# MoE weights of a decoder-layer step: gate/up in two 4 MB slots, four neighbouring rows per partition, down in 2 MB pieces

## The reference, cut to what matters

```
logits = x2d @ w_router + b_router
top_v, top_i = lax.top_k(logits, 4)          # 4 of 32 experts per token
gates = softmax(top_v)
h = xb @ w_gate_up[e] + b_gate_up[e]          # (tokens, 1024) @ (1024, 2048)
x_glu, x_lin = min(h[..., ::2], 7), clip(h[..., 1::2], -7, 7)
h = x_glu * sigmoid(1.702 * x_glu) * (x_lin + 1)
y += gate * (h @ w_down[e] + b_down[e])       # (tokens, 1024) @ (1024, 1024)
```

## Time and profile before

| | |
|---|---|
| median of 3 runs | 1138.27 us (1138.12 to 1141.05) |
| profiled execution, span from first to last instruction | 1140.5 us |
| its own device time | not shown apart; of the three times, 1141.05 us is the one that holds the span |
| TensorE busy | 1027.2 us, 90% |
| VectorE, ScalarE busy | 403.0 us, 206.3 us |
| DMA | 426.10 MB, mean 374 GB/s |
| chain that ended last | PE 80%, DVE 8%, DMA 5%, issue 3%, ACT 3% |

### The profile page before, as it was taken

How to read it: one execution, slowest core, us unless ns; L and a number is a source line. 1 busy time by engine, 2 the same in 40 slices (tenths; PEclk the granted TensorE clock), 3 DMA queues, 4 the chain that set the end, 5 groups by cost and what they waited for, 6 DMA issues and landing times.

```text
span 1140.5 us, 17017 instructions
## 1 busy us (share of the span) xinstructions
PE 1027.2 (90%) x6428; PEld 432.8 (38%) x6428; DVE 403.0 (35%) x886; ACT 206.3 (18%) x440; POOL 7.0 (1%) x7
## 2 busy tenths in 40 slices
PE   6987999999988998899887988789999999999995
PEld 5756875333332323232332233223333333333332
DVE  6978645231322232223222133213333333222223
ACT  4576332111111111111101011101011111111110
POOL 1000000000000000000000000000000000000000
PEclk9978999999999999999999999989999999999998
DMA  9513871999999999999999999999999999999993
GB/s 357 170 47 98 357 308 50 390 423 421 407 417 420 420 421 421 420 419 421 421 421 419 422 420 421 422 420 422 421 422 422 422 421 422 422 422 421 422 420 134
DMA packets 65633, 426.10 MB, mean 374 GB/s; under 512 B 9988, under 2 KB 13188, under 8 KB 15648
## 3 DMA queue, kind: packets, MB, share of 16 engines
q1 hardware_dynamic: 63792, 422.88, 90.2%
q10 hardware_dynamic: 1728, 2.11, 0.5%
q0 software_dynamic: 48, 0.15, 0.0%
HBM read 419.86 MB, written 2.51 MB: 370 GB/s over the span
## 4 chain that ended last, share of the span: by engine, by line
PE 80%; DVE 8%; DMA 5%; issue 3%; ACT 3%; SPq 1%; ACTq 1%; DVEq 0%
PE banks L489 76%; DMA gu_ring<-w_gu_dram 5%; DVE xT L1873 2%; DVE raw L1827 1%; PE banks L855 1%; PE banks L817 1%; ACT gath L1267 1%; PE banks L908 1%; DVE hl L1839 1%; DVE hT L1844 1%; SPq L324 1%; ACT s_p L1170 0%; PE banks L862 0%; PE banks L915 0%; PE banks L624 0%
## 5 line engine op out<-in xcount | busy, mean ns | idle before, releaser
L489 PE MATMUL banks<-gu_ring,xe 128*64 128x512 f32 x1408 | 324.2, 603 | 4.2 <-DMA gu_ring<-w_gu_dram 4.0
L1873 DVE TENSOR_TENSOR xT<-xT,banks 128x576 f32<-128x576 f32 x132 | 93.7, 751 | 488.9 <-PE banks L489 488.9
L489 PEld LDWEIGHTS banks<-gu_ring,xe 128*64 128x64 f32 x1408 | 95.1, 137 | 198.0 <-issue 189.0
L489 PE MATMUL banks<-dn_ring,hT 128*64 128x512 f32 x704 | 157.7, 596 | 3.5 <-DVE hT L1844 3.5
L489 PE MATMUL banks<-gu_ring,xe_s 128*32 128x512 f32 x896 | 110.2, 599 | 11.5 <-issue 6.0
L489 PEld LDWEIGHTS banks<-dn_ring,hT 128*64 128x64 f32 x704 | 47.8, 137 | 94.6 <-issue 88.7
L489 PE MATMUL banks<-gT,ye 64*128 64x288 f32 x352 | 57.8, 439 | 13.4 <-DVE xT L1873 12.7
L1282 ACT ACTIVATE raw<-banks 128x512 f32<-128x512 f32 x22 | 13.1, 597 | 295.5 <-PE banks L489 295.5
L489 PE MATMUL banks<-x_tok,oh 96*64 96x512 f32 x264 | 63.2, 615 | 0.1
L489 PE MATMUL banks<-dn_ring,hT_s 128*32 128x256 f32 x896 | 55.3, 394 | 2.7 <-ACT xe_s L1301 2.7
L1827 DVE COPY raw<-banks 128x512 f32<-128x512 f32 x22 | 15.2, 692 | 109.1 <-PE banks L489 109.1
(11 more groups left out here) (344 smaller groups left out, 838.3 us busy)
## 6 DMA issues: line engine op xcount, KB each, us to landing
gu_ring<-w_gu_dram SPq DMA_DIRECT2D x256, 1024.0 KB, 23.6
dn_ring<-w_dn_dram SPq DMA_DIRECT2D x128, 1024.0 KB, 20.6
w_out<-w_out_dram SPq DMA_DIRECT2D x2, 2048.0 KB, 10.3
w_in<-w_in_dram SPq DMA_DIRECT2D x3, 1024.0 KB, 16.2
w_in<-w_in_dram SPq DMA_DIRECT2D x4, 512.0 KB, 9.7
W<-W1c SPq DMA_DIRECT2D x16, 128.0 KB, 2.3
w_glu<-w_glu_dram SPq DMA_DIRECT2D x1, 2048.0 KB, 8.7
xT<-xT_dram SPq DMA_DIRECT2D x2, 576.0 KB, 5.6
```

The lines of the kernel that those rows point to most:

```text
L489: return nc.tensor.matmul(out, lhsT, rhs, start=start, stop=stop, **kw)
L1873: X.tensor_tensor(two, two, pair[(1, 3)[n % 2]].rearrange("p (h f) -> p h f", h=2)[:, :, 0:T], ALU.add).then_inc(S("acc_done"), 1)
```

## The change

The gate/up weights of an expert come in two pieces of 4 MB instead of eight of 1 MB. Slot k holds rows 512k to 512k+511 of the weights, and partition p of it the four neighbouring rows 512k+4p to 512k+4p+3, which lie one behind the other in DRAM: 32 KB per partition. TensorE contracts row i of all partitions at a time, so a chunk is now every fourth row. Down comes in two pieces of 2 MB with 16 KB per partition, four rows each. TensorE waits for a gate/up slot at chunks 0 and 4 and for a down piece at every second; SP refills a slot after its fourth chunk, a down piece after its second. Places 0 and 1 still get their gate/up weights in 1 MB pieces of 8 KB per partition, and those of place 1 don't wait for `order_ready` any more.

So that the operands match, ScalarE writes `x_tok` with its columns permuted, the copies of the hidden values (`raw`, `raw_s`) put their blocks in another order, and the transposes of the hidden values read every second column. The gate/up bias is permuted once, by four matmuls (`turn_gate_bias`) and a ScalarE copy early in the kernel. The seven early semaphores of `w_in` become their own.

```diff
+GU_SLOTS = 2
+GU_ROWS = KT // GU_SLOTS
...
-    gu_ring = [sb(f"gu_ring{k}", [2 * D], GU + k * 8192) for k in range(8)]
-    dn_ring = [sb(f"dn_ring{k}", [2, D], DN + k * 8192) for k in range(8)]
+    gu_ring = [sb(f"gu_ring{k}", [GU_ROWS, 2 * D], GU + k * GU_ROWS * 8192) for k in range(GU_SLOTS)]
+    dn_ring = [sb(f"dn_ring{k}", [4, D], DN + k * 16384) for k in range(4)]
...
     def load_gu(sp, x, k):
-        sp.dma_start(gu_ring[k][:], a["w_gu"][bass.ds(x, 1), k].rearrange("o p f -> (o p) f")).then_inc(gu_in[k], 16)
...
+        src = a["w_gu"][bass.ds(x, 1), GU_ROWS * k:GU_ROWS * (k + 1)].rearrange("o k p f -> (o k p) f").rearrange(
+            "(p i) f -> p i f", i=GU_ROWS)
+        sp.dma_start(gu_ring[k][:], src).then_inc(gu_in[k], 16)
...
         def gu(x, p_before):
-            for k in range(8):
-                sp.wait_ge(S("gu_used"), p_before * 8 + (k + 1))
+            for k in range(GU_SLOTS):
+                sp.wait_ge(S("gu_used"), p_before * 8 + GU_ROWS * (k + 1))
                 load_gu(sp, x, k)
 
+        def dn(x, p_before, j):
+            for h in range(2):
+                sp.wait_ge(S("dn_used"), p_before * 4 + 2 * (h + 1))
+                load_dn(sp, x, h, j)
+
+        for r in range(KT):
+            sp.wait_ge(S("gu_used"), r + 1)
+            first_gu(sp, 1, [r])
         sp.wait_ge(S("order_ready"), 1)
...
         turn_b(0)
+        turn_gate_bias()
...
             for k in chunks:
-                pe.wait_ge(gu_in[k], p * 16 + (16 + W_IN[k]))
+                slot, i = gu_ring[k // GU_ROWS], k % GU_ROWS
+                if i == 0:
+                    pe.wait_ge(gu_in[k // GU_ROWS], gu_filled(p, k // GU_ROWS))
...
+        def hidden_cols(ap, m):
+
+            return ap.rearrange("p (k n i) -> p k i n", k=2, i=2)[:, m % 2, m // 2]
...
-                    last = pe.transpose(pb[2 + part][:, c * P:(c + 1) * P], raw[:, part, c * P:(c + 1) * P], ident[:])
+                    last = pe.transpose(pb[2 + part][:, c * P:(c + 1) * P], hidden_cols(raw[:, part], c), ident[:])
...
-                pe.wait_ge(dn_in[4 * j + c], fill * 16)
+                if c % 2 == 0:
+                    pe.wait_ge(dn_in[2 * j + c // 2], fill * 16)
...
-            A(x_tok[u // 2][0:MT, (u % 2) * HALF:(u % 2 + 1) * HALF], pb[XB[u]][0:MT, :], ACT.Copy,
+            half = x_tok[u // 2][0:MT, (u % 2) * HALF:(u % 2 + 1) * HALF]
+            A(half.rearrange("p (i f) -> p f i", i=GU_ROWS),
+              pb[XB[u]][0:MT, :].rearrange("p (f i) -> p f i", i=GU_ROWS), ACT.Copy,
...
-            A(raw[:, 0], pb[0][:], ACT.Copy).then_inc(S("g_copied"), 1)
+            A(blocks_out(raw[:, 0]), blocks_in(pb[0]), ACT.Copy).then_inc(S("g_copied"), 1)
```

More of the change, by code:

```diff
@@ L289, in build @@
         S(n)
[L290 to L293, removed]
+    wu_in, wq_in = [S(f"wu_in{c}") for c in range(CT)], [S(f"wq_in{c}") for c in range(3)]
+    gu_in = [S(f"gu_in{k}") for k in range(GU_SLOTS)]
+    dn_in = [S(f"dn_in{k}") for k in range(4)]
     order = {"dve": 0, "act": 0}
@@ L320, in build, with gu_rows, dn_rows, load_dn @@
     assert at == 42
-    def load_gu(sp, x, k):
-        sp.dma_start(gu_ring[k][:], a["w_gu"][bass.ds(x, 1), k].rearrange("o p f -> (o p) f")).then_inc(gu_in[k], 16)
[L326 to L333, removed]
+    def gu_rows(x, k):
+        return a["w_gu"][x, GU_ROWS * k:GU_ROWS * (k + 1)].rearrange("k p f -> (k p) f").rearrange(
+            "(p i) f -> p i f", i=GU_ROWS)
+    def dn_rows(x, h):
+        return a["w_dn"][x, 2 * h:2 * h + 2].rearrange("c p k f -> (c p k) f").rearrange("(p i) f -> p i f", i=4)
+    def load_gu(sp, x, k):
+        src = a["w_gu"][bass.ds(x, 1), GU_ROWS * k:GU_ROWS * (k + 1)].rearrange("o k p f -> (o k p) f").rearrange(
+            "(p i) f -> p i f", i=GU_ROWS)
+        sp.dma_start(gu_ring[k][:], src).then_inc(gu_in[k], 16)
+    def load_dn(sp, x, h, j):
+        src = a["w_dn"][bass.ds(x, 1), 2 * h:2 * h + 2].rearrange("o c p k f -> (o c p k) f").rearrange(
+            "(p i) f -> p i f", i=4)
+        sp.dma_start(dn_ring[2 * j + h][:], src).then_inc(dn_in[2 * j + h], 16)
+    def first_gu(sp, x, rows):
+        for r in rows:
+            k, i = r // GU_ROWS, r % GU_ROWS
+            sp.dma_start(gu_ring[k][:, i], gu_rows(x, k)[:, i]).then_inc(gu_in[k], 16)
+    def gu_filled(p, k):
+        if isinstance(p, int) and p < 2:
+            return 16 * GU_ROWS * (p + 1)
+        return p * 16 + 16 * (2 * GU_ROWS - 1)
+    def blocks_in(ap):
+        return ap.rearrange("p (b k r) -> p b k r", b=2, k=2)
+    def blocks_out(ap):
+        return ap.rearrange("p (k b r) -> p b k r", b=2, k=2)
     def first_dn(sp, j):
-        for c in range(4):
-            sp.dma_start(dn_ring[4 * j + c][:], a["w_dn"][j, c]).then_inc(dn_in[4 * j + c], 16)
+        for h in range(2):
+            sp.dma_start(dn_ring[2 * j + h][:], dn_rows(j, h)).then_inc(dn_in[2 * j + h], 16)
     def load_others(sp):
-        regs = [sp.alloc_register(f"sp_at{k}") for k in range(3)]
+        regs = [sp.alloc_register(f"sp_at{k}") for k in range(2)]
         def expert_at(k, p):
@@ L457, in _ @@
         sp.wait_ge(S("out_done"), 64)
-        first_gu(sp, range(6, 8))
+        first_gu(sp, 0, range(6, 8))
         first_dn(sp, 1)
@@ L650, in values, with turn_gate_bias @@
             last.then_inc(S("pv_ready"), 1)
+        def turn_gate_bias():
+            pe.wait_ge(S("late_in"), 48)
+            pe.wait_ge(S("un_ready"), CT)
+            src = b_gu[:].rearrange("p (g b k) -> p b g k", b=2, k=2)
+            dst = pb[0].rearrange("p (g i k) -> p i g k", i=2, k=2)
+            for i in range(2):
+                for b in range(2):
+                    last = mm(dst[HD * b:HD * b + HD, i], ident[:, i:P:2], src[:, b], True, True,
+                              tile_position=(0, HD * b))
+            last.then_inc(S("bgu_turned"), 1)
         turn_b(0)
+        turn_gate_bias()
         pe.wait_ge(S("v_ready"), 1)
@@ L883, in slim_part @@
                     pe.wait_ge(S("h_s_ready"), s + 1)
-                if kind == "few":
-                    pe.wait_ge(dn_in[4 * j + c], fill * 16)
+                if kind == "few" and c % 2 == 0:
+                    pe.wait_ge(dn_in[2 * j + c // 2], fill * 16)
                 for kk in range(2):
```

59 lines of the change are left out of this document (29 added, 30 removed).

## The result

The changed kernel takes **1153.52 us** (median of 4 runs, 1151.63 to 1158.86) against 1139.66 us of the kernel before beside it: a ratio of 1.0123 (95% interval 1.0100 to 1.0145). Timed again with the last experiments it gave 1154.86 us against 1140.97, ratio 1.0126 (1.0106 to 1.0147). The forecast was 1140.8 us with a range of 1131 to 1150, so the time lies outside it, on the slower side. The profiled execution took 1155.06 us, 1153.3 of them span. Four executions of 1254 to 5204 us (one of the kernel before, one of e11, two of e12) lie far outside all others and are in no median or ratio here.

A forecast was written before the change was run, and what follows sets the result against it. DMA paced the kernel until place 19's weights landed, TensorE from about 770 us. Larger packets (-13.3) and queue idle (+9.3) moved that landing to 759.9; the turn came 1.6 us later, plus 0.9: +2.5, 1140.8 us, range 1131 to 1150.

The forecast's parts named there:

- the second rival: Gate/up and down loads: 32 KB packets move no faster than 8 KB; 11 us slower, 1149.3 us; chance 0.15.
- The same place in the other three rounds: ... by about 1.6 us each: 4.8 us: Down loads behind the `many` experts of the later rounds: the queue, full before, now empties, costing 4.8 us.
- The walk: Step through SP's issues in the old trace to price queue idle from coarse slots: 9.3 us together.
- 1.0 + 1.4 + 4.8 = 7.2: DMA queue behind `many` experts: 1.0 us already thin near 310 us, 1.4 more there, 4.8 in the other rounds.
- 18 x 0.74 = 13.3 us earlier: Weights up to place 19's gate/up: larger packets save 0.74 us per expert over 18 experts, 13.3 us.
- What stands behind the last landing: Place 19: after its weights land, four chunks (6.9 us) and the combine (3.0 us) remain; hidden values turned at 769.9.
- 759.9: Time in us when place 19's weights would be complete: 763.9 - 13.3 + 9.3.
- The copies of `raw` and `x_tok` move as many elements, in runs of 128 or with another step: ScalarE's permuted copies of hidden values and tokens: costed at nothing.
- Such a load takes 140 ns ... I take zero: Stepped weight loads in hidden-value transposes: no extra cost taken; 3.4 us if doubled first loads show, 13 if all exposed.
- The turn of the loop: TensorE idles 1.93 us there, four times; left as is, at most 0.9 us more per turn, 3.6 in all.
- The bias: Four early matmuls, about 1 us, before 4.14 us of idle TensorE: costed at nothing, 1 us once without that cover.
- The third: Rival: TensorE's own path grows, by stepped loads (3.4 us, up to 13) or loop turns; 1144.2 with 3.4; chance 0.18.

The follow-up runs named there:

- e11: The changed kernel without the permutation (weights laid out in DRAM instead), gate/up in eight 1 MB pieces, down in two of 2 MB: 1140.72 us, ratio 0.9996.
- e12: The changed kernel without the permutation (weights laid out in DRAM instead), gate/up in four 2 MB slots, down in 1 MB pieces: 1140.20 us, ratio 0.9987.
- e3: The kernel before, 8 KB packets kept, with TensorE's waits and SP's refills made coarse (four gate/up, two down pieces) and SP's changed loop: 1158.64 us, ratio 1.0151.
- e4: The changed kernel without the permutation: the host lays the weights out in DRAM so that the contraction keeps its old order: 1150.60 us, ratio 1.0080.
- e2: The changed kernel's permuted order, but gate/up and down in 1 MB pieces of 8 KB packets, each waited for and released alone: 1143.97 us, ratio 1.0027.
- e8: e3 with TensorE's waits made fine again, SP's refills still coarse: 1143.39 us, ratio 1.0019.
- e9: e3 with SP's refills made fine again, TensorE's waits still coarse: 1149.35 us, ratio 1.0076.
- e10: e2 with the hidden values' copies and weight loads in the old order, x_tok still permuted; output not the reference's: 1143.41 us, ratio 1.0023.
- e6: The changed kernel with x_tok written in the old column order; output not the reference's: 1154.18 us, ratio 1.0103.
- e15: e10 with x_tok in the old order too; output not the reference's: 1139.01 us, ratio 0.9991.
- e1: The changed kernel with four gate/up slots of two rows (2 MB, 16 KB packets), permuted to fit: 1143.86 us, ratio 1.0033.

## Why the prediction was wrong

The prediction's terms can be held one by one against kernels that have them:

| | forecast | measured |
|---|---|---|
| coarse waits at 8 KB packets (e3) | +11.0, by the second rival: 2.5 + 13.3 - 4.8 | +17.9 |
| large packets on top (e4 against e3) | -13.3 + 4.8 = -8.5 | -8.0 |
| permuted operands (the change against e4; e2 alone) | 0 | +4.0 (e2: +3.2) |
| sum | +2.5 | +13.9 |

- **"The same place in the other three rounds: ... by about 1.6 us each: 4.8 us" failed; it is the largest step.** The walk let the queue empty in the later rounds only because a faster DMA would be ahead by then, and the second rival says that without this the idle of the later rounds "does not arise". In e3 DMA is no faster, and the queue empties in every round: at 393, 372, 370 and 387 GB/s instead of 421 the four stretches lack 11.5 us of transfer, 9.5 of them in the last three rounds, where the rival had none. In the changed kernel they lack 15.3 us at 431 GB/s, where the forecast had 1.0 + 1.4 + 4.8 = 7.2. I had walked through the issues of the trace of before, one by one, with TensorE's releases where they stood there. Such a walk leaves out that a late landing makes TensorE late, which makes the next release late: e8 and e9 alone sum to 11.1 us, near the 11.0 of the walk, together they are 17.9.
- **"18 x 0.74 = 13.3 us earlier" is a price at a full queue, and as such it held.** An expert in 29.1 us is 432 GB/s, and 431 were measured. The prediction took back 4.8 of the 13.3 as longer idle time of the queue; net it has 8.5 us, and the runs give 8.0. How these 8.0 divide into the two no run shows, nor whether so close an agreement is in part luck.
- **"What stands behind the last landing" was right:** 10.0 us forecast from the landing to the turning of the hidden values at place 19, 10.2 in the trace of the change. Only the landing itself was 11.1 us later than 759.9.
- **"The copies of `raw` and `x_tok` move as many elements, in runs of 128 or with another step", costed at nothing, failed, by 2.5 to 3.6 us if the run times are read so.** For `raw` it holds (597 and 692 ns, unchanged). A copy to `x_tok` went from 684 to 1119 ns. Its writes step by 128 elements, 512 bytes. The six copies are 2.6 us longer in sum, of which 0.5 to 0.9 us show on TensorE. The Trainium skill (SBUF — State Buffer, section Door 1) says that every access that crosses to a new 16-byte line pays; the trace agrees, and I had read the same rule only for the step of two.
- **"Such a load takes 140 ns ... I take zero" failed in the price, hardly in the sum.** 207 ns, 0.09 us per place, 1.1 us in the places that show; e10 without it is 0.6 us faster than e2. Where the Trainium skill (the same section) has a step of up to four floats for free, the trace disagrees: with a step of two floats the weight load is half as long again.
- **The turn of the loop**, left as it is, grew. The longest wait with "issue" as its cause is 1.9 to 2.3 us in the eight kernels with 8 KB packets throughout (the one before among them), 2.3 to 2.4 in the four with 16 KB gate/up packets, and 2.9 to 3.7 in the five with 32 KB (e11, with 16 KB for down alone, has 2.2); the means over the three turns stand above. The Trainium skill (DMA: Bandwidth & Descriptors, section Queues, rings and completion order) has a DMA engine change queues at packet borders only; the idle time grows with the packets, as it would by that rule, by 0.6 us per turn on average; but what is awaited there stays unseen, and the longest turns are past the 0.9 us that the prediction took as the most (3.1 against 2.1 us in the change and the kernel before, 3.7 in e6). So the rule is not shown to be the cause. It is part of what e4 loses.
- **The bias** costs nothing, as forecast (e15).

Of the rivals none came alone. The second gave 1149.3 us, the nearest figure, by a cause that wasn't there: 32 KB packets did move faster. The third, TensorE's own path grows, came near the price it named (3.4 us), but through `x_tok` more than through the loads, as far as the run times show. It didn't exclude the forecast: it added to it. I had given each rival as one deviation from the sum; the result was two terms too small, the dry queue by some 7 us and the permutation by 3 to 4, both on the same side, and the range up to 1150 had been made for one.

## What to carry to other kernels

When a transfer is made larger, price the packets and the grain apart, and price the grain on both sides: the reader starts when all has landed, the refill starts when all is used, and here, with a buffer of two pieces, the two losses fed each other (2.6 and 8.5 us alone, 17.9 together). A walk through the old trace must move the releases along with the landings. A gain in bandwidth counts only while the queue is full, so a per-byte saving times all bytes is its upper end. If large packets are wanted, arrange the data in DRAM for them instead of permuting operands on the chip, and stop at the size that is near full rate: here 16 KB in four slots, level with the kernel before, where 32 KB in two lost 0.8% even without the permutation.

## What the hardware showed that I had not expected

- ScalarE copying 96 x 512 floats from PSUM to SBUF takes 684 ns when it writes neighbours and 1119 ns when each element lands 512 bytes from the last (1146 ns in e1, where the writes go to and fro between two places 512 bytes apart).
- A float32 weight load of 128 x 128 takes 140 ns, and 207 with a step of two floats; four transposes in a row grow from 0.66 to 0.74 us, by this row of the changed kernel in order of time:

```profile
841.26 0.74 PE L903 MATMUL banks<-ident,raw 128*128 128x128 f32 x4
```
- Rows 32 KB apart in DRAM, read in 8 KB packets, are as fast as neighbouring ones: 422 GB/s in e2 as in the kernel before (900 to 930 us).
- Refills that SP issues up to four chunks late cost only 2.6 us of 1140 as long as TensorE starts on each 1 MB piece as it lands (e8); with TensorE waiting as coarsely, the same late refills cost 9.3 us (e3 against e9).
- TensorE's granted clock fell to half more often behind the longer idle times at the loop's turns: in 11 of 15 turns after 2.6 us of idle on average, in 5 of 24 after 2.0 us.
